# One hybrid decoder layer on one core: the MLP's two matrix products by seven products per 2x2 quad of blocks

## The chip, the core and the metric

The kernel runs on one core of a Trainium2 chip. It computes one layer of a hybrid decoder in fp32 with inputs and outputs as in the reference, in one launch. The metric is the device time of a launch in microseconds. Five engines work side by side on queues of their own: PE (TensorE, matmuls), DVE (VectorE), ACT (ScalarE), POOL (GpSimd) and SP (SyncE, here only an issuer of DMAs). They meet only in semaphores: each waits until a count is reached. Matmuls write to PSUM, eight banks of 512 fp32 columns per partition; everything else lies in SBUF.

## The reference, cut to what is touched

512 prompt tokens and 32 sample tokens (544 in all) go through the layer. After the three mixers comes

```python
x = x + mix @ w_out_l                       # w_out: 2048 x 2048, its first 512 rows belong to group A
hm = rmsnorm(x, g_mlp)
x = x + jnp.square(jax.nn.relu(hm @ w_up_l)) @ w_down_l
```

with `w_up` of 2048 x 8192 and `w_down` of 8192 x 2048, all fp32. The change touches the last part of the first line (the rows of `w_out` of group A) and the other two lines.

## The kernel before

The stages before `output_and_mlp` (the input projection in its feature-wise and token-wise form, attention, the two scans, their part of the output projection) are not touched. `output_and_mlp` (L3017) holds everything with tokens along the free axis, in two halves of 272 (`HM`), and features along partitions, 128 per tile: `x` and `h` are 16 tiles.

fp32 values go through PE as two fp32r parts: ACT writes the high part of a weight or an activation, another engine the low part (value minus high). A block product is then three matmuls per k-tile: high by high, high by low, low by high. Weights come in chunks of 2048 columns per partition, in two parts of 1024: SP loads a part into `raw` (L3084), ACT writes its high part to `ring` (`highs`, L3313), POOL its low part (`lows`, L3110), PE uses it (L3152). `ring` has two chunks.

The output projection (16 tiles, L3186) adds to `x` (DVE, L3227), multiplies by the gain (L3270), squares (ACT, L3358) and sums the squares by a matmul with ones (L3166); the high and low part of the gained tile become `h`. `rstd` is applied later, behind the up product.

The MLP runs in a hardware loop of 8 groups (`GROUPS`): 8 up chunks, which give 8 tiles of hidden features, then 8 down chunks, which add these 8 tiles' share to all 16 tiles of `x`. An up chunk is 16 k-tiles by 3 matmuls by 2 halves, so 96 matmuls of 128 x 272, and so is a down chunk (8 k-tiles, 2 output tiles). The two halves go to two banks in turn. DVE takes max(0, .) times `rstd` (L3247), ACT squares (L3337), DVE splits the hidden tile (L3235, L3237) into `hid`, which stays in SBUF. The down product is added to `x` by DVE (L3227). The order of each engine is written out by hand; SP's loads wait for `split`, ACT's highs for PE to be done with the ring's slot. At the end PE turns `x` back (L3215), DVE copies it (L3303) and ACT stores it.

## Time and profile before

| | |
|---|---|
| median of 3 runs | 3514.57 us (3513.46 to 3515.31) |
| the profiled execution | 3514.76 us, span 3512.9 us |
| output projection of group A | 1860.0 to 1928.8 us of the span |
| MLP | 1928.8 to 3493.6 us |
| turning back and storing | to 3512.9 us |
| busy: PE, DVE, ACT, POOL | 91%, 40%, 24%, 38% |

Times in a row are microseconds unless marked ns; positions count from the first instruction of the span. A row of groups gives line, engine, operation, output and inputs, shape, count, then busy time, mean ns of one, and the engine's idle time before them with what ended it. Matmuls are pipelined, so one lasts longer in the record than the distance between two starts; the same holds, less so, for DVE and ACT.

### The profile page before, as it was taken

What the parts mean: (1) busy time and instruction counts of PE and PEld (TensorE: products, weight loads), DVE (VectorE), ACT (ScalarE), POOL (GpSimd) and SP (SyncE); (2) the same over time, 40 slices, a digit from 0 to 9 for tenths busy, and PEclk for the clock granted to TensorE, in tenths of its full rate; (3) what the DMA queues carried; (4) which work ended last, traced back from release to release, by engine and by line L of the source; (5) the groups of instructions that cost most, each with busy time, mean ns of one, the idle gap of its engine ahead of it and who ended that gap; (6) DMA issues with size and microseconds to landing.
All of it is one profiled execution on the core that took longest, in us unless ns stands there. A gap on an engine that the chain in (4) does not pass through costs nothing. (4 is left out here: it accounts for less than half of the span.)

```text
span 3512.9 us, 53674 instructions
## 1 busy us (share of the span) xinstructions
PE 3205.1 (91%) x22287; PEld 2954.2 (84%) x22287; DVE 1396.2 (40%) x2390; ACT 843.7 (24%) x1376; POOL 1349.7 (38%) x852
## 2 busy tenths in 40 slices
PE   7968999999984677786998999999999999999998
PEld 6934888999763577745887999999999999999998
DVE  5026975697318665455874211111111111111112
ACT  4222222222317211224323211111121212111120
POOL 4344333475423222313334433334333343433342
PEclk9989999999995788777998999999999999999999
DMA  5322333588743000226424232222232222322222
GB/s 185 99 76 80 106 98 95 143 248 242 223 132 84 20 1 1 82 81 190 120 72 148 86 96 83 87 85 87 82 97 85 85 85 85 93 84 90 85 85 99
DMA packets 415936, 360.25 MB, mean 103 GB/s; under 512 B 26362, under 2 KB 367962, under 8 KB 414309
## 3 DMA queue, kind: packets, MB, share of 16 engines
q1 hardware_dynamic: 380368, 288.60, 28.1%
q0 software_dynamic: 13440, 42.02, 3.9%
q10 hardware_dynamic: 21888, 26.05, 2.1%
q8 instruction: 197, 3.23, 0.4%
q14 instruction: 43, 0.35, 0.0%
HBM read 311.63 MB, written 46.20 MB: 102 GB/s over the span
## 5 line engine op out<-in xcount | busy, mean ns | idle before, releaser
L3110 POOL TENSOR_TENSOR om_ring<-om_raw,om_ring 128x1024 fp32r<-128x1024 f32 x262 | 622.4, 2398 | 950.0 <-ACT om_ring L3313 950.0
L3152 PE MATMUL om_ps<-om_h,om_ring 128*128 128x272 f32 x6144 | 777.5, 289 | 16.7 <-issue 16.6
L3152 PEld LDWEIGHTS om_ps<-om_h,om_ring 128*128 128x128 f32 x6144 | 775.0, 190 | 19.1 <-issue 19.0
L3152 PE MATMUL om_ps<-om_hid,om_ring 128*128 128x272 f32 x6144 | 771.0, 288 | 0.0
L3152 PEld LDWEIGHTS om_ps<-om_hid,om_ring 128*128 128x128 f32 x6144 | 770.2, 189 | 0.0
L3313 ACT ACTIVATE om_ring<-om_raw 128x1024 fp32r<-128x1024 f32 x264 | 264.2, 1048 | 636.5 <-PE om_ps L3152 613.5
L3227 DVE TENSOR_TENSOR om_x<-om_x,om_ps 128x272 f32<-128x272 f32 x288 | 113.0, 434 | 694.8 <-PE om_ps L3152 656.3
L342 POOL TENSOR_TENSOR w_ring<-w_raw,w_ring 128x1024 fp32r<-128x1024 f32 (+2 forms) x110 | 251.7, 2308 | 345.5 <-ACT w_ring L426 345.1
L393 PE MATMUL pm_ps<-h,w_ring 128*128 128x280 f32 x2688 | 356.7, 294 | 9.1 <-issue 8.5
L393 PEld LDWEIGHTS pm_ps<-h,w_ring 128*128 128x128 f32 x2688 | 350.1, 190 | 15.5 <-issue 15.4
L3247 DVE SCALAR_TENSOR_TENSOR om_relu<-om_ps,om_rstd 128x272 f32<-128x272 f32 x128 | 50.4, 436 | 643.9 <-PE om_ps L3152 643.9
L411 PE MATMUL pm_ps<-w_ring,h 128*128 128x512 f32 (+2 forms) x1152 | 238.1, 366 | 8.0 <-POOL w_ring L342 8.0
L411 PEld LDWEIGHTS pm_ps<-w_ring,h 128*128 128x128 f32 x1152 | 200.6, 190 | 41.9 <-issue 8.0
L1961 PE MATMUL ao_w<-ao_mh,ao_ring 128*128 128x272 f32 x1152 | 180.9, 308 | 20.7 <-POOL ao_mh L2101 13.4
L3337 ACT ACTIVATE om_relu<-om_relu 128x272 f32<-128x272 f32 x128 | 49.9, 432 | 622.4 <-DVE om_relu L3247 622.4
L426 ACT ACTIVATE w_ring<-w_raw 128x1024 fp32r<-128x1024 f32 (+2 forms) x128 | 124.8, 1011 | 275.6 <-PE as_dead_bank L411 177.4
L1961 PEld LDWEIGHTS ao_w<-ao_mh,ao_ring 128*128 128x128 f32 x1152 | 156.4, 193 | 37.1 <-issue 18.4
L2111 POOL TENSOR_TENSOR ao_ring<-ao_raw,ao_ring 128x768 fp32r<-128x768 f32 x32 | 60.8, 1920 | 123.0 <-ACT ao_ring L2045 123.0
L2714 POOL DMA_INDIRECT as_rows<-in_cache_v,as_offs x64 | 64.8, 1012 | 96.1 <-PE as_o_bank L2978 81.1
L393 PEld LDWEIGHTS pi_ps<-h,w_ring 128*128 128x128 f32 x768 | 98.5, 188 | 0.1
L393 PE MATMUL pi_ps<-h,w_ring 128*128 128x280 f32 x768 | 98.5, 290 | 0.0
L2833 DVE TENSOR_TENSOR as_prod<-as_rows,as_qb 128x512 f32<-128x512 f32 x64 | 95.7, 1495 | 0.0
(527 smaller groups left out, 3515.6 us busy)
## 6 DMA issues: line engine op xcount, KB each, us to landing
om_raw<-in_w_up SPq DMA_DIRECT2D x128, 512.0 KB, 4.2
om_raw<-in_w_down SPq DMA_DIRECT2D x128, 512.0 KB, 3.7
w_raw<-in_w_in SPq DMA_DIRECT2D x112, 512.0 KB, 3.9
ao_raw<-in_w_out SPq DMA_DIRECT2D x32, 384.0 KB, 3.8
...
```

The lines of the kernel that those rows point to most:

```text
L342: eng.tensor_tensor(f32r(ring[:, n % 2, 1, half_of(q, n)]), raw[:, q, whole(q, n)], ring[:, n % 2, 0, half_of(q, n)], ALU.subtract).then_i ...
L393: ins = pe.matmul(bank_of(b + y)[:, 0:HALF], piece(a, k), f32r(h[:, x, k, two_halves(y)]), start=first, stop=last)
L411: ins = pe.matmul(bank_of(b + m)[:, 0:w], f32r(h[:, x, ld.k0 + k, tok]), piece(a, k), start=first, stop=last)
L426: act.activation(f32r(ring[:, n % 2, 0, half_of(q, n)]), raw[:, q, whole(q, n)], ACT.Copy).then_inc(hi_ready[q], 1)
L1961: ins = pe.matmul(w_ps[2 * (n % 2) + half][:, 0:HM], w, f32r(mh[:, b, k, kept_half(half)]), start=first, stop=last)
L2111: pool.tensor_tensor(f32r(ring[:, n % 2, 1, half_of(q)]), raw[:, q, :], ring[:, n % 2, 0, half_of(q)], ALU.subtract).then_inc(split[q], 1)
L2714: pool.indirect_dma_start(self.rows[:, n % RING, :], None, table, bass.IndirectOffsetOnAxis(ap=self.offs[:, x, j:j + 1], axis=0)).then_inc ...
L2833: dve.tensor_tensor(prod[:, n % 2, :], self.rows[:, n % RING, :], self.qb[:, j % 4, :], ALU.mult).then_inc(s["multiplied"], 1)
L3110: pool.tensor_tensor(f32r(ring[:, s, 1, half_of(q)]), raw[:, q, :], ring[:, s, 0, half_of(q)], ALU.subtract).then_inc(split[q], 1)
L3152: ins = pe.matmul(ps[bank][:, 0:HM], w, f32r(src[:, b, k, kept_half(half)]), start=first, stop=last)
L3227: dve.tensor_tensor(dst, dst, ps[b][:, 0:HM], ALU.add).then_inc(evac[b], 1)
L3313: act.activation(f32r(ring[:, s, 0, half_of(q)]), raw[:, q, :], ACT.Copy).then_inc(hi_ready[q], 1)
```

## The change

The weight matrices are cut into 2x2 quads of blocks, the activations into 2x2 as well: even and odd k-tiles by first and second half of the tokens. A quad's product is then made of seven block products by the scheme with 7 instead of 8 products (Winograd's form), which needs four sums of weight blocks (S1 = 21 + 22, S2 = S1 - 11, S4 = 12 - S2, and S3 = 11 - 21) and four of activation blocks per quad, and joins the products in PSUM or on DVE. There are 32 quads in the up product (`UPS`) and 8 groups of 4 in the down product (`IPS`), `QUADS` = 64. Everything is straight-line code; the loop over groups is gone. The whole up product comes first, then the whole down product.

A weight block is a piece of 1024 columns. Pieces come in the order `NAMES` (11, 12, S2, S1, S3, S4, 22). ACT writes a piece's high part and DVE, no longer POOL, its low part; `ring` has three slots of one piece. S1, S2 and S4 are made by DVE, S3 by POOL, which does nothing else. `raw` has six slots that change their roles from quad to quad, so S1 takes the place of the 12 of the quad before, and S3 that of its own 21.

In the up product ACT copies five partial sums from PSUM per quad, DVE makes three joins, applies `rstd` and max (1088 columns at once), ACT squares, DVE makes four differences, ACT and DVE split seven blocks (272 and 1632 columns), and SP stores the quad's seven split blocks to a DRAM buffer (`hid`, 1.95 MB per quad). In the down product SP loads them back by groups (`load_hidden`, seven loads of 1.11 MB per group) into the place of the activations' seven block combinations `hc`, and DVE adds every product to two tiles' halves of `x` (544 columns, `gather`). The hidden blocks of a quad pass through rows of `x`, so three quarters of `x` are stored behind the output projection and loaded again at the start of the down product. In the output projection DVE and ACT also prepare the seven combinations per pair of tiles (`combos`, `combo_lows`, `plain_highs`, `combo_highs`), all by DVE and ACT, none by POOL. The closing part is the same but for three instead of two staging buffers.

The diff, cut to its core (`done` is the product three pieces back, whose result an engine fetches before it makes piece n):

```diff
--- before.py
+++ after.py
-GROUPS, GT = 8, FF // 8 // P
-PER = GT * P // 128
+PIECE = 1024
+OUT_PIECES = D // (2 * P)
+UPS = FF // (2 * P)
+GJ = 4
+GROUPS = UPS // GJ
+IPS = D // (4 * P)
+QUADS = UPS + GROUPS * IPS
+SLOTS = 3
+NAMES = ("11", "12", "S2", "S1", "S3", "S4", "22")
+MOVES = (0, 1, 4, 3, 5, 2, 6)
+HOMES = (((0, 0), (0, 1), (1, 0), (1, 1), (4, 0), (4, 1), (3, 0)), ((5, 0), (5, 1), (2, 0), (2, 1), (6, 0), (6, 1), (3, 1)))
+H11, H12, H21, H22, HT = 0, 1, 2, 3, 4
+def piece(q, idx):
+    return OUT_PIECES + 7 * q + idx
+def raw_slots():
+    at = {"11": 2, "12": 0, "21": 1, "22": 3, "sum": 4, "spare": 5}
+    out = []
+    for _ in range(QUADS):
+        out.append(at)
+        at = {"11": at["spare"], "12": at["11"], "21": at["sum"], "22": at["21"], "sum": at["12"], "spare": at["22"]}
+    return out
...
+        def bank_of(q, idx):
+            return {1: 2, 3: 4, 5: 4}.get(idx, alpha(q))
...
+            def loads(q):
+                if q >= 2:
+                    sp.wait_ge(lo, piece(q - 2, 6) + 1)
...
+                load(q, "11")
+                sp.wait_ge(lo, piece(q - 1, 2) + 1 if q else 7)
+                load(q, "12")
+                sp.wait_ge(lo, piece(q - 1, 3) + 1 if q else 8)
+                load(q, "21")
+                if q:
+                    sp.wait_ge(lo, piece(q - 1, 4) + 1)
+                else:
+                    sp.wait_ge(prepared, 8)
+                load(q, "22")
+            def store_hidden(j):
+                sp.wait_ge(h_lo, 2 * (j + 1))
+                for a in range(2):
+                    sp.dma_start(hid[:, j // GJ, :, a, j % GJ, :], hsplit[:, a, :, :]).then_inc(hid_out, 16)
+            def load_hidden(g, c):
+                slot, half = home(g, c)
+                if g < 2:
+                    sp.wait_ge(product, 7 * (UPS - 1) + MOVES.index(slot) + 1)
+                else:
+                    sp.wait_ge(product, 7 * (UPS + IPS * (g - 1) - 1) + MOVES.index(c) + 1)
+                sp.wait_ge(hid_out, 32 * GJ * (g + 1))
+                sp.dma_start(hc[:, slot, :, GJ * half:GJ * (half + 1), :], hid[:, g, c, :, :, :]).then_inc(hid_in[g % 2][c], 16)
...
+            for q in range(QUADS):
+                loads(q)
+                if q == 0:
+                    sp.wait_ge(added, 16)
+                    sp.dma_start(x_t[:, 12:16, META:], x[:, 12:16, :]).then_inc(x_saved[3], 16)
+                if 2 <= q < UPS + 2:
+                    store_hidden(q - 2)
+                if q == UPS + 1:
+                    sp.wait_ge(x_saved[1], 16)
+                    sp.dma_start(x[:, 4:8, :], x_t[:, 4:8, META:]).then_inc(x_back[1], 16)
+                if q == UPS + 2:
+                    for part in (2, 3):
+                        sp.wait_ge(x_saved[part], 16)
+                        sp.wait_ge(hid_out, 32 * UPS)
+                        sp.dma_start(x[:, 4 * part:4 * part + 4, :], x_t[:, 4 * part:4 * part + 4, META:]
+                                     ).then_inc(x_back[part], 16)
+                if q == UPS:
+                    for c in MOVES:
+                        load_hidden(0, c)
+                g, phase = divmod(q - UPS - 1, IPS)
+                if q > UPS and g + 1 < GROUPS and phase < 3:
+                    for c in (MOVES[0:2], MOVES[2:4], MOVES[4:7])[phase]:
+                        load_hidden(g + 1, c)
...
-            def lows(n, s):
-                for q in range(PARTS):
-                    pool.wait_ge(hi_ready[q], n + 1)
-                    pool.tensor_tensor(f32r(ring[:, s, 1, half_of(q)]), raw[:, q, :], ring[:, s, 0, half_of(q)], ALU.subtract
-                                       ).then_inc(split[q], 1)
...
+            def bank_ready(q, idx):
+                up, b = q < UPS, 7 * (q - UPS)
+                if idx == 0:
+                    if q == 0:
+                        pe.wait_ge(added, KT)
+                    elif q == 1:
+                        pe.wait_ge(rooted, 1)
+                    elif q < UPS + 2:
+                        pe.wait_ge(copied, 5 * (q - 2) + 5)
+                    else:
+                        pe.wait_ge(gathered, b - 14 + 7)
+                elif idx == 1 and q:
+                    pe.wait_ge(joined, 3 * (q - 1) + 1) if q <= UPS else pe.wait_ge(gathered, b - 7 + 2)
+                elif idx == 2:
+                    pe.wait_ge(copied, 5 * q + 1) if up else pe.wait_ge(gathered, b + 1)
+                elif idx == 3 and q:
+                    pe.wait_ge(joined, 3 * (q - 1) + 3) if q <= UPS else pe.wait_ge(gathered, b - 7 + 6)
+                elif idx == 4:
+                    pe.wait_ge(copied, 5 * q + 2) if up else pe.wait_ge(gathered, b + 3)
+                elif idx == 5:
+                    pe.wait_ge(copied, 5 * q + 3) if up else pe.wait_ge(gathered, b + 4)
+                elif idx == 6:
+                    pe.wait_ge(copied, 5 * q + 4) if up else pe.wait_ge(gathered, b + 5)
+            def up_product(q, idx):
+                n, c = piece(q, idx), MOVES[idx]
+                pe.wait_ge(lo, n + 1)
+                bank_ready(q, idx)
+                for k in range(8):
+                    if q == 0 and idx == 0:
+                        pe.wait_ge(prepared, k + 1)
+                    for a, b in ((0, 0), (0, 1), (1, 0)):
+                        last = pe.matmul(ps[:, bank_of(q, idx), 0:HM], f32r(ring[:, n % SLOTS, a, P * k:P * (k + 1)]),
+                                         f32r(hc[:, c, b, k, :]), start=(idx in (0, 1, 3) and k == a == b == 0),
+                                         stop=(idx in (1, 5, 6) and k == 7 and a == 1), skip_group_check=True)
+                last.then_inc(product, 1)
+            def down_product(q, idx):
+                n, c = piece(q, idx), MOVES[idx]
+                g, ip = divmod(q - UPS, IPS)
+                slot, half = home(g, c)
+                pe.wait_ge(lo, n + 1)
+                bank_ready(q, idx)
+                if ip == 0:
+                    pe.wait_ge(hid_in[g % 2][c], 16 * (g // 2 + 1))
+                for i in range(2):
+                    for j in range(GJ):
                         for a, b in ((0, 0), (0, 1), (1, 0)):
...
+                            w = f32r(ring[:, n % SLOTS, a, 2 * P * j + P * i:2 * P * j + P * (i + 1)])
+                            last = pe.matmul(ps[:, bank_of(q, idx) + i, 0:HM], w, f32r(hc[:, slot, b, GJ * half + j, :]),
+                                             start=(idx in (0, 1, 3) and j == a == b == 0),
+                                             stop=(idx in (1, 5, 6) and j == GJ - 1 and a == 1), skip_group_check=True)
+                last.then_inc(product, 1)
...
+            def low(n):
+                dve.wait_ge(hi, n + 1)
+                dve.tensor_tensor(f32r(ring[:, n % SLOTS, 1, :]), source(n), ring[:, n % SLOTS, 0, :], ALU.subtract
+                                  ).then_inc(lo, 1)
+            def sums(q, which):
+                at = {name: raw[:, slot, :] for name, slot in slots[q].items()}
+                arrived = lambda name: dve.wait_ge(raw_in[slots[q][name]], landed[q, name])
+                if which == "S1":
+                    if q:
+                        dve.wait_ge(lo, piece(q - 1, 5) + 1)
                     else:
...
+                        dve.wait_ge(prepared, 8)
+                    arrived("21")
+                    arrived("22")
+                    dve.tensor_tensor(at["sum"], at["21"], at["22"], ALU.add).then_inc(s_done, 1)
+                elif which == "S2":
+                    dve.wait_ge(s_done, 3 * q + 1)
+                    dve.wait_ge(s3_done, q + 1)
+                    dve.wait_ge(lo, piece(q, 0) + 1)
+                    dve.tensor_tensor(at["11"], at["sum"], at["11"], ALU.subtract).then_inc(s_done, 1)
+                else:
+                    dve.wait_ge(s_done, 3 * q + 2)
+                    dve.wait_ge(lo, piece(q, 1) + 1)
+                    dve.tensor_tensor(at["12"], at["12"], at["11"], ALU.subtract).then_inc(s_done, 1)
...
+            def hidden_scaled(q):
+                dve.wait_ge(copied, 5 * q + 5)
+                dve.wait_ge(joined, 3 * q + 3)
+                both = hs[:, 0:4, :].rearrange("p (m a) t -> p m (a t)", m=2)
+                dve.scalar_tensor_tensor(out=both, in0=both, scalar=0.0, in1=bc(rstd.unsqueeze(1), [P, 2, TM]), op0=ALU.max,
+                                         op1=ALU.mult).then_inc(scaled, 1)
+            def hidden_combos(q):
+                dve.wait_ge(squared, q + 1)
+                dve.tensor_tensor(hs[:, HT, :], hs[:, H12, :], hs[:, H11, :], ALU.subtract).then_inc(h_made, 1)
...
+            def hidden_lows(q):
+                dve.wait_ge(h_hi, 2 * q + 2)
+                dve.tensor_tensor(f32r(hsplit[:, 1, 0, :]), hs[:, 0, :], hsplit[:, 0, 0, :], ALU.subtract).then_inc(h_lo, 1)
+                dve.tensor_tensor(f32r(hsplit[:, 1, 1:7, :]), hs[:, 2:8, :], hsplit[:, 0, 1:7, :], ALU.subtract
+                                  ).then_inc(h_lo, 1)
...
+            for n in range(OUT_PIECES):
+                add_tile(2 * n)
+                low(n + 2)
+                add_tile(2 * n + 1)
+                combos(n)
+                combo_lows(n)
+            for n in range(piece(0, 2), piece(QUADS, 3)):
+                q, idx = divmod(n - OUT_PIECES, 7)
+                done_q, done = divmod(n - OUT_PIECES - 3, 7)
+                if 0 <= done_q < UPS:
+                    if done in (4, 5):
+                        if done == 4:
+                            join(done_q, 1)
+                        join(done_q, done)
+                elif done_q >= UPS:
+                    gather(done_q, done)
+                if q < QUADS:
+                    if q == 0 and idx == 2:
+                        sums(0, "S1")
+                        sums(0, "S2")
+                    elif q and idx == 0:
+                        sums(q, "S1")
+                    elif q and idx == 1:
+                        sums(q, "S2")
+                    if idx == 2:
+                        sums(q, "S4")
+                if 1 <= q <= UPS and idx == 5:
+                    hidden_combos(q - 1)
+                if q < QUADS:
+                    low(n)
+                if q == 0 and idx == 4:
+                    dve.wait_ge(rooted, 1)
+                    dve.reciprocal(rstd, rstd).then_inc(rstd_ready, 1)
+                    dve.wait_ge(rstd_ready, 1)
+                if 1 <= q <= UPS and idx == 3:
+                    hidden_scaled(q - 1)
+                if 1 <= q <= UPS and idx == 6:
+                    hidden_lows(q - 1)
...
+        @block.gpsimd
+        def _(pool):
+            for q in range(QUADS):
+                at = {name: raw[:, slot, :] for name, slot in slots[q].items()}
+                pool.wait_ge(s_done, 3 * q + 1)
+                pool.wait_ge(raw_in[slots[q]["11"]], landed[q, "11"])
+                pool.tensor_tensor(at["21"], at["11"], at["21"], ALU.subtract).then_inc(s3_done, 1)
...
+            def high(n):
+                slot_free(act, n)
+                source_ready(act, n)
+                act.activation(f32r(ring[:, n % SLOTS, 0, :]), source(n), ACT.Copy).then_inc(hi, 1)
...
+            for n in range(OUT_PIECES):
+                square(2 * n)
+                high(n + 2)
+                square(2 * n + 1)
+                plain_highs(n)
+                combo_highs(n)
+            act.wait_ge(summed, KT)
+            act.activation(rstd.rearrange("p (a t) -> p a t", a=2), ps[:, 6:8, 0:HM], ACT.Sqrt, bias=sb["eps"][:, 0:1],
+                           scale=1.0 / D).then_inc(rooted, 1)
+            for n in range(piece(0, 2), piece(QUADS, 3)):
+                q, idx = divmod(n - OUT_PIECES, 7)
+                done_q, done = divmod(n - OUT_PIECES - 3, 7)
+                if 0 <= done_q < UPS and done in (0, 2, 3, 4, 6):
+                    copy_out(done_q, done)
+                if q < QUADS:
+                    high(n)
+                if 1 <= q <= UPS and idx == 4:
+                    hidden_squares(q - 1)
+                if 1 <= q <= UPS and idx == 5:
+                    hidden_highs(q - 1)
```

## Rows read from the trace of the kernel before

**Rows 1.** The page: busy time of each engine, and the clock by slices.

```profile
PE 3205.1 (91%) x22287; PEld 2954.2 (84%) x22287; DVE 1396.2 (40%) x2390; ACT 843.7 (24%) x1376; POOL 1349.7 (38%) x852
PEclk9989999999995788777998999999999999999999
```

**Rows 2.** Stretches: from:to, length, busy of each engine (x instructions), PEclk, DMA share, GB/s.

```profile
2125.00:2320.00 195.00, 192.90 (x1532) 192.69 (x1531) 30.05 (x80) 37.47 (x48) 74.71 (x33) 0.99 0.29 87
```

**Rows 3.** Waits in 1929 to 3493: engine, line, awaited, us in total, times, longest.

```profile
DVE om_x L3227 <- PE om_ps L3152: 656.3, 128, 5.2
...
PE om_ps L3152 <- issue: 16.6, 10, 2.3
```

**Rows 4.** PE in order of time: start, length, what, idle before.

```profile
1859.98 11.26 PE L3186 MATMUL om_ps<-om_h,om_ring 128*128 128x272 f32 x72 [14.50 <-POOL om_h L3116]
...
1890.83 1.08 PE L3166 MATMUL om_ps<-om_tile,ones 128*128 128x272 f32 x4
...
1894.76 1.08 PE L3166 MATMUL om_ps<-om_tile,ones 128*128 128x272 f32 x4
...
1928.85 96.57 PE L3152 MATMUL om_ps<-om_h,om_ring 128*128 128x272 f32 x768
2025.26 96.37 PE L3152 MATMUL om_ps<-om_hid,om_ring 128*128 128x272 f32 x768
2123.63 98.01 PE L3152 MATMUL om_ps<-om_h,om_ring 128*128 128x272 f32 x768 [2.00 <-issue]
...
2319.94 2.51 PE L3152 MATMUL om_ps<-om_h,om_ring 128*128 128x272 f32 x18 [2.10 <-issue]
...
3493.58 7.18 PE L3215 MATMUL om_ps<-ident,om_x 128*128 128x128 f32 x64 [0.84 <-DVE om_x L3227]
```

**Rows 5.** A stretch of L411 alone, columns PE and PEld, clock, DMA share, GB/s.

```profile
60.00:70.00 10.00, 10.00 (x45) 8.16 (x44) 1.00 0.14 35
```

**Rows 6.** DVE: two of 1024 and of 272 columns in a row, then means of one.

```profile
888.45 2.36 DVE L342 TENSOR_TENSOR w_ring<-w_raw,w_ring 128x1024 fp32r<-128x1024 f32 x2 [6.81 <-ACT w_ring L426]
1941.14 0.79 DVE L3247 SCALAR_TENSOR_TENSOR om_relu<-om_ps,om_rstd 128x272 f32<-128x272 f32 x2 [2.37 <-PE om_ps L3152]
...
L342 DVE TENSOR_TENSOR w_ring<-w_raw,w_ring 128x1024 fp32r<-128x1024 f32 x18 | 21.3, 1220 | 95.9 <-ACT w_ring L426 78.9 <-issue 17.0
L3247 DVE SCALAR_TENSOR_TENSOR om_relu<-om_ps,om_rstd 128x272 f32<-128x272 f32 x128 | 50.4, 436 | 643.9 <-PE om_ps L3152 643.9
```

**Rows 7.** ACT: two of 1024 and of 272 columns, and a hand-off to DVE.

```profile
1935.01 2.00 ACT L3313 ACTIVATE om_ring<-om_raw 128x1024 fp32r<-128x1024 f32 x2
1941.62 0.78 ACT L3337 ACTIVATE om_relu<-om_relu 128x272 f32<-128x272 f32 x2 [4.60 <-DVE om_relu L3247]
...
874.37 1.06 ACT L426 ACTIVATE w_ring<-w_raw 128x1024 fp32r<-128x1024 f32 x1 [5.03 <-DMA w_raw<-in_w_in]
875.56 1.23 DVE L342 TENSOR_TENSOR w_ring<-w_raw,w_ring 128x1024 fp32r<-128x1024 f32 x1 [4.14 <-ACT w_ring L426]
```

**Rows 8.** A DVE product alone and beside POOL; POOL's 1024 columns (mean ns).

```profile
783.76 0.68 DVE L2833 TENSOR_TENSOR as_prod<-as_rows,as_qb 128x512 f32<-128x512 f32 x1
785.08 5.88 DVE L2833 TENSOR_TENSOR as_prod<-as_rows,as_qb 128x512 f32<-128x512 f32 x1
785.68 4.73 POOL L342 TENSOR_TENSOR w_ring<-w_raw,w_ring 128x1024 fp32r<-128x1024 f32 x2
...
L3110 POOL TENSOR_TENSOR om_ring<-om_raw,om_ring 128x1024 fp32r<-128x1024 f32 x262 | 622.4, 2398 | 950.0 <-ACT om_ring L3313 950.0
```

**Rows 9.** DMA: a stretch while x is loaded, and the landing of a weight load.

```profile
1864.00:1866.00 2.00, 2.00 (x16) 2.00 (x16) 0.78 (x2) 0.00 (x0) 0.00 (x0) 0.90 1.06 390
om_raw<-in_w_up SPq DMA_DIRECT2D x128, 512.0 KB, 4.2
```

**Rows 10.** Stretches as in rows 2: behind the gap at 2121, and behind that at 2318.

```profile
2125.00:2126.00 1.00, 1.00 (x6) 1.00 (x6) 0.00 (x0) 0.00 (x0) 1.00 (x2) 0.50 0.00 0
2323.00:2325.00 2.00, 2.00 (x18) 2.00 (x18) 0.00 (x0) 0.00 (x0) 0.83 (x1) 1.00 0.86 245
```

518 lines of the change are left out of this document (256 added, 262 removed).

## The prediction

> **What bounds the kernel now.** I read the page's busy times first [rows 1], then the stages [rows 2], then who waits for whom in the MLP [rows 3], and last TensorE's own order of time [rows 4]. The page says PE 91% busy, every other engine at most 40%. In the MLP a stretch of 195 us holds 193 us of PE at full clock, with DVE at 30 us, ACT at 37 and POOL at 75. The waits agree: DVE waited 656 us for PE; PE waited 16.6 us in all, for "issue". So PE sets the end. 768 matmuls take 96.37 us with the tail of the last; their starts are 0.1253 us apart. Out of 1564.7 us between the first MLP matmul (1928.85) and the first transpose (3493.58) the 12288 matmuls are 1539.7. The other 25 lie at the group loop's seven boundaries, about 2 us of "issue" each, after some of which the clock drops.
>
> **PE's side of the change.** A quad of 2x2 blocks needed 8 block products and now needs 7: 8 k-tiles by 3 split terms by 7 are 168 matmuls of the same shape, where the same 256 rows and 544 tokens took 192. 64 quads make 10752, which is 1536 fewer: -192.4 us. A product lasts 24 x 0.1253 = 3.01 us, a quad 21.04, all 64 1346.8. The loops are gone, and straight-line PE code elsewhere shows no such gaps, so the 25 us go too. One thing is new to this stage: the 12 or 24 matmuls in a row that go to one bank, where before two banks alternated. The input projection's token-wise branch (L411) already sends 12 in a row of 512 columns to one bank and does 45 in 10 us, 0.222 us each [rows 5]. That is 9 ns over the columns' own 0.213 at 2.4 GHz, where the 272-column matmuls show 12 over 0.113. So I cost it at nothing; that row bounds it closely from both sides.
>
> **What the other engines must do in a quad.** Two DVE operations of 1024 columns take 2.36 us, one 1.22: starts are 1.14 us apart, and for 272 columns 0.36 (0.79 less 0.43) [rows 6]. A line through both gives 0.64 for 544, 1.21 for 1088 and 1.77 for 1632 (estimates). ACT: 0.95 for 1024, 0.35 for 272, so 1.0 for 1088 and 1.44 for 1632 [rows 7]. From an ACT end to the DVE start that waits for it 0.13 us pass (875.43 to 875.56) [rows 7].
> The weight lows move from POOL to DVE. In an up quad DVE does 7 lows and 3 sums (10 x 1.14), 3 joins (1.08), the scaling (1.21), 4 differences of the hidden blocks (1.44) and the hidden lows (0.36 + 1.77): 17.3 us. In a down quad it is 10 x 1.14 and 7 gathers of 0.64: 15.9. POOL does one sum, 2.40 us [rows 8].
> POOL and DVE get in each other's way. A DVE product of two SBUF tiles takes 0.68 us alone; one that meets two POOL operations (4.73 us) takes 5.88, 5.20 more [rows 8]. DVE stood still for as long as POOL worked, and a little over. So POOL's 2.40 go on DVE's time in each quad where both want to work. The bounds are 0 (POOL meets only DVE's idle time) and 2.6 (half of 5.20); I take 2.40, POOL's own length, as that row is near it.
> Down quads then have 18.3 of 21.04 us, and a ring of three slots lets DVE run two products (6 us) ahead: hidden. Up quads have 19.7, so what counts is the order.
>
> **An up quad in DVE's order**, every operation starting when its engine is free and its last wait is met; t = 0 at S1. S1 to 1.14, low 11 to 2.29. POOL, ready at 1.35, gets in when that low is through, 2.29 to 4.69. DVE meanwhile has only a 0.36 join and waits 2.17 for S3. S2 at 4.82, low 12 at 5.96, S4 at 7.22 (it waits 0.12 for its predecessor's end), the lows of S2 and S1 at 8.36 and 9.50, the scaling at 10.64, low S3 at 11.85. The differences wait for ACT's square (12.06 to 13.15), start at 13.29 and are through at 15.0; low S4 15.12. ACT then splits the hidden blocks (0.35 + 1.44), copies a bank (0.35) and only then makes the high of 22 (17.2 to 18.2), so its low starts at 18.36, after 2.10 of waiting. Hidden lows 19.5 to 21.6, two joins, next S1 at 22.47. Work 17.26 and waits 5.2: the ring of DVE, POOL and ACT closes in 22.47 us without any wait for PE, which needs 21.04. PE then waits 1.43 us in each up quad, at its second product, for low 12. The Trainium skill (VectorE: DVE Perf Modes, "The DRAIN you can't avoid") says that after every operation the next starts only when the pipe is empty. The pair of [rows 6] shows starts 1.14 apart with 1.22 of length, so the measurement decides; by that sentence the ring would be about 1.5 us longer (0.08 for each of 19 operations), +45 us in all.
>
> **The stages.** (a) Output projection. PE needs 3.93 us per tile (1890.83 to 1894.76), 62.8 in all, and before took 68.9 (1859.98 to 1928.85) [rows 4]. Now ACT and DVE work by pairs of tiles on one chain: add, square, base copy, four dependent differences, ACT's split, its low (1.21), the next add, its square, ACT's high and the low of the weights: 0.73 + 0.7 + 0.5 + 1.7 + 1.4 + 1.2, then 0.85 + 0.7 + 1.1 + 1.2, about 10.1 us per pair where PE needs 7.86. The first two tiles (7), eight such chains (80.8) and less the last one's tail (3.3), behind whose first parts the MLP already starts: 84.5 us, +15.6.
> (b) First up quad: S1, S2 and S4 can start only after the last preparation (buffers shared with it), with POOL's 2.4 between. PE waits 8.4 us before its third product and 1.7 for the last tile of the first: +10.0.
> (c) 30 further up quads' stalls: +43 (30 x 1.43).
> (d) Turn to the down product: the first group's hidden blocks, 7 x 1.11 MB, go out only behind the store of hidden 30 (1.95 MB). At the 390 GB/s that the load of x reached [rows 9] the first lands 7.0 us late, each next one in 2.9, under a product's 3.0. The weights of the second down quad stand behind them: +4.0 and +2.4. Sum +13.4.
> (e) Down quads: none, +1.1 at the last gather.
> (f) Clock. After two of the gaps of some 2 us the clock is 0.5 for 3.4 us, and the stretch took 98.01 us instead of 96.57; after that of 2319 it stayed up [rows 4, 10]. I charge 8 us for the gaps of (a), (b) and (d), most of one such loss for each, and none for the stalls of 1.43 us in (c), which are shorter than any gap of these rows.
> Everything before L3017, and the 19.3 us of transposes and stores behind it, stay. DMA: before 86 GB/s in the MLP. Per quad now 2.1 MB of weights and 1.95 MB of hidden blocks, first out and later in: 192 GB/s of the 390, and DVE needs the last weight block 6 us after its issue where one lands in 4.2 [rows 9]: nothing.
>
> **Sum.** -192.4 - 25.2 + 15.6 + 10.0 + 43 + 13.4 + 1.1 + 8 = -126.5; walked through without rounding, -127.2. The profiled execution is 3514.76 us (span 3512.9), 0.2 over the median of 3514.57. So 3387.6 by its time, 3387.4 against the median: I say 3388.
>
> **Rivals.** (1) *The up quads run at PE's pace.* If POOL's sum meets no DVE work (DVE is idle for 2.2 us around it) and hand-offs are shorter, the ring falls to 21.3: -1.2 x 30 = -36, and most of (f): 3345. For it: 5.2 us of DVE's ring are waits. Against: DVE's low follows S1 at once, so the two meet each time. Chance 0.20.
> (2) *The stalls cost the clock.* The Trainium skill (TensorE: Matmul & The Clock Gate, "A second HAM failure mode: psum-queue depth-cycling") tells of a kernel whose short idle times between groups made the clock swing. As a mechanism here: each of the 30 stalls drops the clock as the gap at 2121 did [rows 4, 10], 1.44 us each: +43, 3431. Against: 1.4 us is shorter than the gaps seen, and one shown there cost nothing. By that rule of the Trainium skill the swing would be the rule here too; the rows show one gap with it and one without. Chance 0.17.
> (3) *Slower than before.* The same stall, but the half clock holds on. The gain of 127 us is used up when an up quad takes 4.2 us more, so when PE is at 1.2 GHz for over 8.4 us of it. At four of seven products (12 us): +6.0 x 30 = +180, 3568. For it: the middle of the profile has slices at 0.5 and 0.7 [rows 1], 88 us each. Against: PE is nearly idle there, and here it would be 94% busy. Chance 0.05.
> The forecast (ring of 22 to 23 us) keeps 0.56, 3365 to 3410. The last 0.02 is for a transfer or buffer that I have missed.
> **Range.** 3345 (rival 1) to 3433 (just over rival 2), which leaves out rival 3 and the tails. This kernel's runs differ by 0.05%, and about 0.2% can be told from no change. Faster 0.93, same 0.01, slower 0.06.
>
> **What would show it.** In the profile of the changed kernel: 10752 MLP matmuls, 0.125 us apart; DVE near 85% busy in the up stage; PE's starts per up quad 22.5 us apart with one wait per quad, for DVE's low, at the second product; the down stage without waits, 21.04 per quad; DVE waiting for POOL's sum once a quad; some 7 us of PE waiting for a DMA at the turn; full clock in the up stage. It would be wrong if DVE's wait for POOL were absent (rival 1), if PEclk showed 0.5 every quad (2, 3), or if PE waited for DMA in every quad.

## The result, and the profile after

The changed kernel takes 3374.97 us (median of 4 runs, 3372.2 to 3379.66), the kernel before 3514.02 beside it: ratio 0.961 with a 95% interval of 0.959 to 0.963, faster by 139 us. The prediction was 3388, range 3345 to 3433. The profiled execution has a span of 3373.4 us (3375.16 with what lies around it).

The page of the changed kernel: busy times, TensorE's clock by slices; then groups (line, engine, operation, names, shapes, count | busy us, mean ns | idle before them).

```profile
PE 3037.0 (90%) x20751; PEld 2771.9 (82%) x20751; DVE 2270.1 (67%) x2961; ACT 1165.6 (35%) x1713; POOL 924.1 (27%) x643
PEclk9989999999996588957999999999999999999999
...
L3278 PE MATMUL om_ps<-om_hc,om_ring 128*128 128x272 f32 x5376 | 688.6, 290 | 27.6 <-DVE om_ring L3326 27.6
L3295 PE MATMUL om_ps<-om_hc,om_ring 128*128 128x272 f32 x5376 | 685.3, 290 | 12.1 <-DMA om_hc<-hid_scratch 6.6 <-DVE om_ring L3326 2.6 <-DVE om_x L3438 2.5
```

Against [rows 1], PE has 1536 matmuls less and 168 us less to do, and is still 90% busy. DVE has taken over the weight lows: 1396 to 2270 us. The up product (L3278) and the down product (L3295) have the 10752 matmuls predicted, and PE waits 27.6 and 12.1 us in them.

PE in order of time (start, length, what, idle before), the changed kernel, as in [rows 4]:

```profile
1856.60 11.22 PE L3241 MATMUL om_ps<-om_hc,om_ring 128*128 128x272 f32 x72 [15.41 <-DVE om_ring L3326]
...
1886.59 1.19 PE L3225 MATMUL om_ps<-om_small,ones 128*128 128x272 f32 x4 [1.72 <-ACT om_small L3515]
...
1941.14 7.32 PE L3278 MATMUL om_ps<-om_hc,om_ring 128*128 128x272 f32 x48
1957.08 40.92 PE L3278 MATMUL om_ps<-om_hc,om_ring 128*128 128x272 f32 x312 [8.62 <-DVE om_ring L3326]
...
2219.63 21.45 PE L3278 MATMUL om_ps<-om_hc,om_ring 128*128 128x272 f32 x168 [0.62 <-DVE om_ring L3326]
2241.69 21.45 PE L3278 MATMUL om_ps<-om_hc,om_ring 128*128 128x272 f32 x168 [0.62 <-DVE om_ring L3326]
...
2663.91 21.12 PE L3295 MATMUL om_ps<-om_hc,om_ring 128*128 128x272 f32 x144 [6.59 <-DMA om_hc<-hid_scratch]
2685.22 3.26 PE L3295 MATMUL om_ps<-om_hc,om_ring 128*128 128x272 f32 x24 [0.20 <-issue]
2689.65 3.29 PE L3295 MATMUL om_ps<-om_hc,om_ring 128*128 128x272 f32 x24 [1.17 <-DVE om_ring L3326]
2694.35 3.29 PE L3295 MATMUL om_ps<-om_hc,om_ring 128*128 128x272 f32 x24 [1.41 <-DVE om_ring L3326]
2697.98 127.80 PE L3295 MATMUL om_ps<-om_hc,om_ring 128*128 128x272 f32 x1008 [0.34 <-DVE om_x L3438]
...
3355.52 8.95 PE L3318 MATMUL om_ps<-ident,om_x 128*128 128x128 f32 x80 [0.81 <-DVE om_x L3438]
```

The output projection lasts 84.54 us (1856.60 to 1941.14); PE waits about every 10 us there, for ACT's squares. Then comes one wait of 8.62 us before the third product. The rows 2219.63 and 2241.69 are two of 29 of their kind: an up quad every 22.07 us, with one wait, for DVE. At the turn to the down product PE waits for the first hidden blocks and then for DVE, and after that for almost nothing: the last two rows are 657.5 us apart.

What DVE and POOL do at the start of an up quad:

```profile
2230.38 1.23 DVE L3326 TENSOR_TENSOR om_ring<-om_raw,om_ring 128x1024 fp32r<-128x1024 f32 x1 [1.80 <-ACT om_ring L3509]
...
2234.57 1.22 DVE L3339 TENSOR_TENSOR om_raw<-om_raw 128x1024 f32<-128x1024 f32 x1
2235.71 1.22 DVE L3326 TENSOR_TENSOR om_ring<-om_raw,om_ring 128x1024 fp32r<-128x1024 f32 x1
2235.87 3.32 POOL L3502 TENSOR_TENSOR om_raw<-om_raw 128x1024 f32<-128x1024 f32 x1 [18.75 <-DVE om_raw L3339]
2236.84 0.43 DVE L3404 TENSOR_TENSOR om_x<-om_ps,om_small 128x272 f32<-128x272 f32 x1
2239.28 1.23 DVE L3344 TENSOR_TENSOR om_raw<-om_raw 128x1024 f32<-128x1024 f32 x1 [2.00 <-POOL om_raw L3502]
2240.42 1.22 DVE L3326 TENSOR_TENSOR om_ring<-om_raw,om_ring 128x1024 fp32r<-128x1024 f32 x1
2241.69 0.52 PE L3278 MATMUL om_ps<-om_hc,om_ring 128*128 128x272 f32 x2 [0.62 <-DVE om_ring L3326]
```

POOL's sum (L3502) has a length of 3.32 us, where 1024 columns took 2.40 [rows 8]: it begins beside DVE's low and gets its turn when that low is through (2236.93). S2 (L3344) waits 2.00 us for it, the low behind S2 is the low of 12, and PE's wait ends when that one ends.

### The profile page after: what moved, and what is told of

Read it like the earlier page. It is cut to its first block and busy times, and to the rows that moved or that the text cites. A ratio compares the mean times of both kernels' runs of the same rounds, so it can differ in the third digit from the quotient of the medians.

```text
span 3373.4 us, 51215 instructions
## 1 busy us (share of the span) xinstructions
PE 3037.0 (90%) x20751; PEld 2771.9 (82%) x20751; DVE 2270.1 (67%) x2961; ACT 1165.6 (35%) x1713; POOL 924.1 (27%) x643
## 5 line engine op out<-in xcount | busy, mean ns | idle before, releaser
L3278 PE MATMUL om_ps<-om_hc,om_ring 128*128 128x272 f32 x5376 | 688.6, 290 | 27.6 <-DVE om_ring L3326 27.6
L3278 PEld LDWEIGHTS om_ps<-om_hc,om_ring 128*128 128x128 f32 x5376 | 681.5, 189 | 34.7 <-DVE om_ring L3326 34.4
L3509 ACT ACTIVATE om_ring<-om_raw 128x1024 fp32r<-128x1024 f32 x456 | 482.7, 1059 | 656.1 <-PE om_ps L3295 349.2
L3295 PE MATMUL om_ps<-om_hc,om_ring 128*128 128x272 f32 x5376 | 685.3, 290 | 12.1 <-DMA om_hc<-hid_scratch 6.6
L3295 PEld LDWEIGHTS om_ps<-om_hc,om_ring 128*128 128x128 f32 x5376 | 681.6, 189 | 15.8 <-DVE om_ring L3326 10.2
L3326 DVE TENSOR_TENSOR om_ring<-om_raw,om_ring 128x1024 fp32r<-128x1024 f32 x456 | 554.3, 1221 | 110.3 <-ACT om_ring L3509 110.1
L3502 POOL TENSOR_TENSOR om_raw<-om_raw 128x1024 f32<-128x1024 f32 x64 | 211.2, 3300 | 1297.6 <-DVE om_raw L3339 1297.6
L411 PE MATMUL pm_ps<-w_ring,h 128*128 128x512 f32 (+2 forms) x1152 | 237.3, 365 | 8.0 <-POOL w_ring L342 8.0
L411 PEld LDWEIGHTS pm_ps<-w_ring,h 128*128 128x128 f32 x1152 | 199.9, 189 | 41.9 <-issue 8.1
L3438 DVE TENSOR_TENSOR om_x<-om_x,om_ps 128x544 f32<-128x544 f32 x224 | 160.9, 718 | 75.9 <-PE om_ps L3295 75.4
L3344 DVE TENSOR_TENSOR om_raw<-om_raw 128x1024 f32<-128x1024 f32 x64 | 78.5, 1226 | 117.7 <-POOL om_raw L3502 117.7
L453 ACT ACTIVATE pm_stage<-pm_ps 128x280 f32<-128x280 f32 (+3 forms) x80 | 35.6, 445 | 239.6 <-PE pm_ps L393 189.1
L740 DVE SCALAR_TENSOR_TENSOR conv_y<-conv_x,conv_par,conv_y 128x616 f32<-128x616 f32 x84 | 71.3, 859 | 36.4 <-ACT conv_y L667 34.3
```

The costliest lines, as they stand in the source:

```text
L411: ins = pe.matmul(bank_of(b + m)[:, 0:w], f32r(h[:, x, ld.k0 + k, tok]), piece(a, k), start=first, stop=last)
L3278: last = pe.matmul(ps[:, bank_of(q, idx), 0:HM], f32r(ring[:, n % SLOTS, a, P * k:P * (k + 1)]), f32r(hc[:, c, b, k, :]), start=(idx in (0 ...
L3295: last = pe.matmul(ps[:, bank_of(q, idx) + i, 0:HM], w, f32r(hc[:, slot, b, GJ * half + j, :]), start=(idx in (0, 1, 3) and j == a == b == 0),
L3326: dve.tensor_tensor(f32r(ring[:, n % SLOTS, 1, :]), source(n), ring[:, n % SLOTS, 0, :], ALU.subtract).then_inc(lo, 1)
L3344: dve.tensor_tensor(at["11"], at["sum"], at["11"], ALU.subtract).then_inc(s_done, 1)
L3438: dve.tensor_tensor(dst, dst, ps[:, b:b + 2, 0:HM], ALU.add).then_inc(gathered, 1)
```

## The experiments

They ran in three sets, on different chips, where the kernel before took 3510.89, 3496.39 and 3501.06 us. So ratios to the kernel before of the same set are compared, and rows of the profiles.

| kernel | median us | ratio | 95% interval |
|---|---|---|---|
| changed kernel | 3374.97 | 0.961 | 0.959 to 0.963 |
| the same again (after_again) | 3363.29 | 0.961 | 0.959 to 0.963 |
| before_one_bank | 3512.14 | 1.001 | 1.000 to 1.002 |
| low12_first | 3368.31 | 0.959 | 0.958 to 0.961 |
| s3_on_dve | 3342.2 | 0.952 | 0.950 to 0.954 |
| pool_more | 3404.05 | 0.969 | 0.968 to 0.971 |
| pool_in_four | 3379.13 | 0.965 | 0.964 to 0.967 |
| front_order | 3344.7 | 0.956 | 0.954 to 0.958 |
| turn_order | 3360.24 | 0.961 | 0.959 to 0.963 |
| banks_in_turn | 3355.83 | 0.960 | 0.959 to 0.962 |
| no_round_trip | 3346.8 | 0.957 | one run |
| gains_pool_sum | 3326.89 | 0.950 | 0.949 to 0.952 |
| all_gains | 3309.13 | 0.946 | 0.944 to 0.947 |

**The theory** was that DVE, POOL and ACT form a ring that closes in about 22 us, where PE needs 21, because POOL's sum and DVE keep each other out. **The rival** was that the up quads lose their time elsewhere. Its simplest test takes POOL out.

```diff
                 elif which == "S2":
                     dve.wait_ge(s_done, 3 * q + 1)
+                    arrived("11")
+                    dve.tensor_tensor(at["21"], at["11"], at["21"], ALU.subtract).then_inc(s3_done, 1)
                     dve.wait_ge(s3_done, q + 1)
...
-                pool.tensor_tensor(at["21"], at["11"], at["21"], ALU.subtract).then_inc(s3_done, 1)
```

> The fourth sum S3 is made by DVE too, POOL does nothing in the MLP. Ring theory with POOL and DVE excluding each other: the 2.0 us wait for POOL goes, 1.14 of work comes, the ring falls to 21.2 us and PE (168 x 0.1267 = 21.3) sets the up quad: 30 x 0.78 = 23 us less, 3352; down quads unchanged. Rival (DVE's amount of work sets the up quad, POOL relieves it): 1.14 us more per up quad, 30 x 1.14 = +34, 3409.

Measured 0.952. PE's order of time, all four sums on DVE:

```profile
1951.44 675.05 PE L3278 MATMUL om_ps<-om_hc,om_ring 128*128 128x272 f32 x5328 [6.38 <-DVE om_ring L3326]
2633.08 20.33 PE L3295 MATMUL om_ps<-om_hc,om_ring 128*128 128x272 f32 x144 [6.59 <-DMA om_hc<-hid_scratch]
...
2666.75 651.13 PE L3295 MATMUL om_ps<-om_hc,om_ring 128*128 128x272 f32 x5160 [0.34 <-DVE om_x L3440]
```

The up product is one run of 5328 matmuls with no wait, and by its matmul starts a quad takes 21.23 us instead of 22.07. DVE has one operation more per quad and the kernel is faster. The up part became 25 us shorter (23 expected). That the down part also became 6 us shorter was not expected. In the changed kernel an unstalled down quad takes 21.19 us, but 11 of the 30 quads from the third on take 0.1 to 0.8 us more, 5.7 us in all, at their second and third products. In each of these 11, S1 (L3339) had waited 0.48 to 1.20 us for its weights, and the quad lost that wait less 0.35 to 0.38 us. The waits of the changed kernel and of no_round_trip (below), which keeps POOL's sum but moves less data:

```profile
DVE om_raw L3339 <- DMA om_raw<-in_w_down: 12.4, 14, 2.1
...
DVE om_raw L3339 <- DMA om_raw<-in_w_down: 1.2, 1, 1.2
```

So two things have to meet: weights that land late and POOL's sum on the way from S1 to S2. Without POOL's sum S1 still waits, 9 times between 2710 and 3320 us, and only one quad loses time, 0.16 us; with POOL's sum but without most of the traffic, one loses 0.8 and no other any.

**Which way around the ring.** If POOL's length is what counts, giving DVE other work meanwhile (the low of 12 ahead of S2, which does not need S3) gains little.

```diff
-                    elif q and idx == 1:
-                        sums(q, "S2")
...
                     low(n)
+                    if q and idx == 1:
+                        sums(q, "S2")
```

> DVE makes the low part of block 12 ahead of the sum S2, for which it waits for POOL; nothing else changes. Ring theory (the up quad's 22.07 us are the closed ring of DVE, POOL and ACT; PE's own need is 21.3): the low has two SBUF inputs and so stands still while POOL works, the ring keeps its length, up quads stay at 22.07 us and the time at 3375; PE's wait only changes its place. Rival (PE is held up by that one low): its wait of 0.6 us at the second product goes, up quads take 21.3, 30 x 0.78 = 23 us less: 3352.

Measured 21.86 us per up quad, 0.21 less, where the theory expected none and the rival 0.78. DVE and POOL in that kernel:

```profile
2213.18 1.22 DVE L3326 TENSOR_TENSOR om_ring<-om_raw,om_ring 128x1024 fp32r<-128x1024 f32 x1
2213.34 3.31 POOL L3502 TENSOR_TENSOR om_raw<-om_raw 128x1024 f32<-128x1024 f32 x1 [18.55 <-DVE om_raw L3339]
2214.31 0.43 DVE L3404 TENSOR_TENSOR om_x<-om_ps,om_small 128x272 f32<-128x272 f32 x1
2214.66 3.07 DVE L3326 TENSOR_TENSOR om_ring<-om_raw,om_ring 128x1024 fp32r<-128x1024 f32 x1
2217.66 1.21 DVE L3344 TENSOR_TENSOR om_raw<-om_raw 128x1024 f32<-128x1024 f32 x1
```

The low ahead of S2 takes 3.07 us instead of 1.22: it stands still until POOL ends at 2216.65, and 1.1 us later it is done. DVE's wait for POOL's semaphore became a stop at POOL's operation. The join (L3404), which reads PSUM and a small tile, ran its usual 0.43 beside it.

**How much of a POOL operation counts.** Five more POOL products of 128 columns per quad, on tiles that nothing else needs in the MLP, with no DVE operation waiting for them:

```diff
+                pool.wait_ge(s_done, 3 * q + 3)
+                pool.wait_ge(rooted, 1)
+                for i in range(5):
+                    pool.wait_ge(spun, 5 * q + i)
+                    pool.tensor_tensor(sb["ones"][:, :], sb["ident"][:, :], sb["ident"][:, :], ALU.mult).then_inc(spun, 1)
```

> POOL does five extra products of 128 columns per quad after S4 (about 0.45 to 0.5 us each, 2.4 in all), into a tile nobody reads in the MLP; no engine waits for them. Exclusion theory: DVE's two-input operations stand still for those 2.4 us, the ring becomes 24.4 us: +2.4 x 31 = +73, and down quads (18.3 + 2.4 of 21.3 us) 0 to +10: 3448 to 3458. Rival (POOL costs DVE only the wait for S3): no change, 3375.

Measured 0.969, or 29 us more, and up quads of 22.93 us (+0.87): neither theory's number. DVE and POOL in that kernel:

```profile
2185.36 5.96 POOL L3508 TENSOR_TENSOR ones<-ident 128x128 f32<-128x128 f32 x5 [3.86 <-DVE om_raw L3348]
2187.68 1.48 DVE L3410 SCALAR_TENSOR_TENSOR om_x<-om_x,om_small 128x1088 f32<-128x1088 f32 x1
...
2190.42 0.63 DVE L3415 TENSOR_TENSOR om_x<-om_x 128x272 f32<-128x272 f32 x1
```

DVE's scaling takes 1.48 us where it took 1.29, a difference of the hidden blocks 0.63 for 0.44: each POOL operation costs DVE 0.19 to 0.20. And POOL's five need 5.96 us, 1.19 each: each ends 0.26 us after the DVE operation that it stood behind. The two take turns by whole operations, and what DVE loses is not POOL's whole length but what POOL still has to do when DVE's next operation starts (0.34 us here), less 0.14; neither theory had that. The low of low12_first fits as well: POOL had 1.99 us left at its start, and it took 1.85 longer. The next kernel asks it directly, with the low of 12 ahead of S2 and POOL's sum cut in four (the waits for it count four times as far):

```diff
-                pool.tensor_tensor(at["21"], at["11"], at["21"], ALU.subtract).then_inc(s3_done, 1)
+                for c in range(4):
+                    s = slice(256 * c, 256 * (c + 1))
+                    pool.tensor_tensor(at["21"][:, s], at["11"][:, s], at["21"][:, s], ALU.subtract).then_inc(s3_done, 1)
```

> POOL's sum in four pieces of 256 columns instead of one of 1024, and DVE's low of 12 ahead of its sum S2, so that two lows run beside POOL's pieces. In the kernel with the low ahead and POOL's sum in one piece, the low took 3.07 us beside it instead of 1.22, and the five small POOL operations of another run stretched DVE's by 0.2 us each. Theory (the engines exclude each other for as long as a POOL operation really works, 0.6 to 0.75 us for 256 columns): the lows take 1.9 to 2.0 us beside each piece, DVE loses as much in all, POOL ends later for the four starts, up quads of 21.9 to 22.4 us. Rival (a small POOL operation costs DVE some 0.2 us, whatever its length, and the two take turns): the lows take under 1.5 us each beside POOL, and quads fall to 21.3 to 21.6 us.

DVE and POOL in that kernel:

```profile
2207.84 1.22 DVE L3326 TENSOR_TENSOR om_ring<-om_raw,om_ring 128x1024 fp32r<-128x1024 f32 x1
2208.00 4.72 POOL L3504 TENSOR_TENSOR om_raw<-om_raw 128x256 f32<-128x256 f32 x4 [17.63 <-DVE om_raw L3339]
2208.98 0.43 DVE L3404 TENSOR_TENSOR om_x<-om_ps,om_small 128x272 f32<-128x272 f32 x1
2209.33 1.41 DVE L3326 TENSOR_TENSOR om_ring<-om_raw,om_ring 128x1024 fp32r<-128x1024 f32 x1
...
2212.82 1.23 DVE L3344 TENSOR_TENSOR om_raw<-om_raw 128x1024 f32<-128x1024 f32 x1 [2.08 <-issue]
```

Each theory got one number right. The low beside the pieces takes 1.41 us, not 3.07 or 1.9 (the rival's "under 1.5"): the first piece has 0.33 us left when it starts, again 0.14 more than it loses; but the quads are 22.35 us apart, inside the theory's 21.9 to 22.4. The four pieces together take 4.72 us instead of 3.31: the first two are 1.66 and 1.72 long, since each waits through a DVE low, the last two 0.74 each with DVE idle. What DVE no longer loses by standing still, it loses by waiting 2.08 us for the later S3. The exclusion costs whichever engine has to stand back, and here both ways end at S2.

**The cadence of the matmuls.** In the changed kernel matmuls within a product start 0.1261 us apart, where the kernel before had 0.1253. I had costed sending 12 or 24 in a row to one bank at nothing. The kernel before with the halves as an outer loop does that (and uses the same weights for two matmuls in a row instead of four):

```diff
-                for m in range(cols // P):
+                for m, half in ((m, half) for m in range(cols // P) for half in range(2)):
```

> The kernel before with the halves as the outer loop of a chunk, so that each bank gets its 24 or 48 matmuls in a row and every matmul has other weights than the one before; same matmuls, same count. If one bank in a row (or new weights each time) is why the MLP matmuls now start 0.1267 instead of 0.1253 us apart: 12288 x 0.0013 = +16 us, 3531. Rival (the cadence comes from the heavier DMA and DVE traffic): starts stay 0.1253 us apart, 3514.

1.0006 (0.9996 to 1.0015), starts 0.1256 apart: 0.3 ns of the 0.8. The change's own down product with its two banks in turn, instead of one after the other:

```diff
-                for i in range(2):
-                    for j in range(GJ):
-                        for a, b in ((0, 0), (0, 1), (1, 0)):
+                for j in range(GJ):
+                    for a, b in ((0, 0), (0, 1), (1, 0)):
+                        for i in range(2):
```

> In the down product the two output tiles of a k-tile alternate, so that every matmul goes to the other bank than the one before, with the same moving data twice; same matmuls. After the one-bank run of the kernel before (0.1256 us from 0.1253) I expect of the banks 0.3 ns of the 0.9 by which starts lie further apart than before: down starts at 0.1258, 2 us less, which the total does not show: 3373. If the banks are the whole cause: 0.1253, 5 us less. If traffic is: 0.1261 as now.

Starts in the down product 0.1251 apart instead of 0.1261, and the stage from 2647.64 to 3333.11 takes 685.5 us instead of 691.6. The ratio, 0.960 against 0.961, does not tell 6 us from nothing by itself; the rows do. So in the down product this order of the loop is the whole of the 0.8 ns and 0.2 more, while in the kernel before the swap gave 0.3. That it is the banks is not shown: each of the two edits also changes the order of the operands. Here two matmuls in a row had the same weights, and now none have, while the same moving tile comes twice in a row. No kernel here separates the two.

**The stages with a one-time cost.** In the output projection DVE and ACT put the tile that PE waits for first, ahead of the ring's low and after the ring's high:

```diff
                 add_tile(2 * n)
-                low(n + 2)
                 add_tile(2 * n + 1)
+                low(n + 2)
...
-                square(2 * n)
                 high(n + 2)
+                square(2 * n)
                 square(2 * n + 1)
```

> In the output projection DVE adds both tiles of a pair before it makes the low part of the weights, and ACT makes the weights' high part ahead of the squares. Chain theory (DVE and ACT hand each other the work by pairs in 9.8 us where PE needs 7.8): the square, the high and the low leave the chain, a pair takes PE's 7.8, and the stage falls from 84.5 to about 71 us: 13 less, 3362. Rival (PE waits because DVE is short of time in this stage): its work is unchanged, so the stage stays at 84 and the time at 3375.

0.956 against 0.961, and by the rows the projection takes 67.1 us instead of 84.5:

```profile
1843.87 11.27 PE L3241 MATMUL om_ps<-om_hc,om_ring 128*128 128x272 f32 x72 [15.12 <-DVE om_ring L3326]
...
1910.95 3.01 PE L3278 MATMUL om_ps<-om_hc,om_ring 128*128 128x272 f32 x21
```

The chain of about 10 us per pair was a matter of order, not of work: all 15.6 us that the prediction charged there were to be had back. 17 us came back where I expected 13; how much of it is DVE's swap and how much ACT's is not separated.

At the turn, the loads of the first hidden blocks go ahead of the last-but-one store:

```diff
+                if q == UPS:
+                    for c in MOVES:
+                        load_hidden(0, c)
                 if 2 <= q < UPS + 2:
                     store_hidden(q - 2)
...
-                if q == UPS:
-                    for c in MOVES:
-                        load_hidden(0, c)
```

> At the turn from the up to the down product SP issues the first group's seven loads of hidden blocks ahead of the store of hidden 30. Queue theory (the first load stands behind 1.95 MB of stores, 5 us at 390 GB/s): PE's wait for the first load falls from 6.6 to about 2 us, 5 less in all: 3370. Rival (the load waits for its own buffer, that is for PE): 6.6 us stay, 3375.

No difference in the ratio. PE's order of time in that kernel:

```profile
2645.31 3.19 PE L3295 MATMUL om_ps<-om_hc,om_ring 128*128 128x272 f32 x24
2649.12 15.49 PE L3295 MATMUL om_ps<-om_hc,om_ring 128*128 128x272 f32 x120 [0.62 <-DVE om_ring L3326]
2671.35 11.79 PE L3295 MATMUL om_ps<-om_hc,om_ring 128*128 128x272 f32 x72 [6.74 <-issue]
```

The wait for the first block is gone, and one of 6.74 us has come six products later: from the end of the up product to the transposes it is 695.1 us instead of 698.2. "issue" hides what ended it; ACT and DVE in the same stretch show it:

```profile
2664.41 0.43 ACT L3558 ACTIVATE om_x<-om_x 128x272 fp32r<-128x272 f32 x1 [7.78 <-DMA hid_scratch<-om_x]
...
2667.27 1.23 DVE L3326 TENSOR_TENSOR om_ring<-om_raw,om_ring 128x1024 fp32r<-128x1024 f32 x1 [7.08 <-ACT om_ring L3509]
...
2670.54 0.71 DVE L3438 TENSOR_TENSOR om_x<-om_x,om_ps 128x544 f32<-128x544 f32 x1
```

ACT may split the last hidden blocks only when the store of hidden 30 has left their place. That store now stands behind the 7.8 MB of loads, so ACT waits 7.78 us for it; ACT's highs, DVE's low and DVE's gather (L3438) come later by as much, and PE goes on when that gather is done. The edit moved the wait from the loads to the store; a store that goes between the loads was not tried. That the wait comes from transfers shows with the round trip cut down (one of seven stored blocks and an eighth of each load are kept, so most hidden values that the down product reads are left out):

```diff
-sp.dma_start(hid[:, j // GJ, :, a, j % GJ, :], hsplit[:, a, :, :])
+sp.dma_start(hid[:, j // GJ, 0:1, a, j % GJ, :], hsplit[:, a, 0:1, :])
...
-sp.dma_start(hc[:, slot, :, GJ * half:GJ * (half + 1), :], hid[:, g, c, :, :, :])
+sp.dma_start(hc[:, slot, 0:1, GJ * half:GJ * half + 1, :], hid[:, g, 0, 0:1, 0:1, :])
```

> One seventh of each hidden store and one eighth of each hidden load are left, the rest is left out (the down product then works on old blocks, so the output is not the reference's); waits and order stay. DMA goes from 192 to about 110 GB/s. If the traffic is why the MLP matmuls start 0.9 ns further apart: 0.1253, 8 us less, and with PE's waits at the turn gone (6.6 and 2.8) 3358. If it is not: only the turn's 9 us, 3366.

PE waits 0.62, 0.80, 0.64, 0.34 and 0.33 us at the turn there, and the up quads are 22.07 us apart as before: the round trip costs its 7 us at the turn and nothing in the up stage. Behind the turn PE has no wait left, though POOL makes its sum:

```profile
2697.39 629.78 PE L3295 MATMUL om_ps<-om_hc,om_ring 128*128 128x272 f32 x4992 [0.33 <-DVE om_x L3438]
```

Its matmuls start 0.1261 apart, so the transfers are not what stretches them.

**All together.** The changed kernel again, and two kernels with the gains combined: all_gains has s3_on_dve, front_order, turn_order and banks_in_turn; gains_pool_sum has low12_first in the place of s3_on_dve.

> The changed kernel itself, unaltered, for a comparison on the same chip with the three kernels beside it, since the time of the kernel before differed by 14 us between the earlier sets of runs (3510.89 and 3496.39). Expected: a ratio to the kernel before of 0.961 within 0.002, quads of the up product 22.07 us apart, matmuls of the down product 0.1262 us apart.

> The same with the one change that POOL keeps its sum per quad, DVE's low of 12 going ahead of its sum S2: what is left against the kernel with all four sums on DVE is then the price of POOL's work. Theory (POOL's sum holds DVE's ring, 30 up quads of 21.86 us where PE needs 21.2): 20 us slower in the up stage and level in the down stage, 3375 - 6 - 17 - 3 - 6 = 3343, ratio 0.952. Rival (the gain of moving the sum was the one-time wait before the third product and the smoother down stage, not the ring): ratio below 0.949 and up quads under 21.5 us.

> Four edits together: all four weight sums on DVE, the preparation's new order on DVE and ACT, the loads of the first hidden blocks issued ahead of the store of hidden 30, and the two banks in turn in the down product. If each gain lies in a stretch of its own they add up: 32 us for the sums, 17 for the preparation, 6 for the banks, 3 for the turn; but of the sums' 32, some 6 were waits of 0.2 us per quad in the down stage that two banks in turn could hide or lay bare again, since PE is then faster. Expected 3375 - 52 to 58 = 3317 to 3323, ratio 0.945 to 0.947. Rival: with PE waiting for nothing, DVE's own work of 19 to 20 us per down quad (11 operations of 1.14, 7 gathers) comes within 1 us of PE's 21.0 and PE waits again for DVE: ratio 0.950, with waits for DVE in the down stage. At no time should an up quad take over 21.3 us.

Measured 0.961, 0.950 and 0.946. The changed kernel has up quads of 22.07 us again; gains_pool_sum has 21.86, the theory's number and not the rival's under 21.5. PE's order of time in all_gains:

```profile
1926.97 675.68 PE L3278 MATMUL om_ps<-om_hc,om_ring 128*128 128x272 f32 x5328 [7.43 <-DVE om_ring L3326]
2602.49 18.35 PE L3295 MATMUL om_ps<-om_hc,om_ring 128*128 128x272 f32 x144
2629.27 138.16 PE L3295 MATMUL om_ps<-om_hc,om_ring 128*128 128x272 f32 x1080 [8.42 <-issue]
2767.65 519.30 PE L3295 MATMUL om_ps<-om_hc,om_ring 128*128 128x272 f32 x4152 [0.22 <-DVE om_x L3440]
```

After its first 15 us the MLP has one long wait left, at the turn: 8.42 us, while ACT waits 9.39 us for the store of hidden 30, as in turn_order. From the first matmul of the output projection to the transposes it is 1442.9 us against 1498.9 in the changed kernel: 56 less, in the 52 to 58 expected. The rival (DVE as the bound of the down stage) is out: 5232 matmuls, 0.22 us of waiting. Of the two, the kernel that leaves POOL its sum is 17.8 us slower (20 expected); its down stage, expected level, is 3.8 us longer in the profiled executions. all_gains, at 0.946, is the best of the case.

## Why the prediction was right

The sign, the mechanism and the size came out. The sum did so partly by luck: steps that were too long by 23 us and others too short by 11 leave 12. By its steps, in us of the profiled executions (predicted span 3512.9 - 127.2 = 3385.7, measured 3373.4, so 12.3 too long; waits are taken from start to start, beyond the usual step):

| step | predicted | measured | error |
|---|---|---|---|
| start of the output projection | 1859.98 | 1856.60 | -3.4 |
| (a) output projection | 84.5 | 84.5 | 0.0 |
| (b) waits of the first up quad | 10.0 | 9.6 | -0.4 |
| (c) each of 30 up quads | 22.47 | 22.07, the first 22.41 | -11.7 |
| (d) waits at the turn | 13.4 | 11.0 | -2.4 |
| (e) each of the 34 other quads | 21.04 | 21.19 | +5.1 |
| (e) waits in the 30 last down quads | 0 | 5.7 | +5.7 |
| (e) last gather | 1.1 | 1.0 | -0.1 |
| (f) clock | 8 | 4.2 | -3.8 |
| transposes and stores | 19.3 | 17.9 | -1.4 |

They add up to -12.4. The first is no part of the change: in front_order the same instruction starts at 1843.87.

**The ring** (c) was the argument that decided between 3345 and 3388, and it held to 2%. The order is as walked through: the low first, POOL when it is through, S2 4.71 us after S1 (4.82 predicted), DVE's second wait at ACT's high of 22. That wait was 1.80 us, not 2.10. Set beside the walk-through, DVE is 0.11 us ahead at S2, 0.23 at the differences, 0.48 at the low of 22 and 0.40 at the next S1. s3_on_dve showed the cause: take POOL's sum away, and the ring is faster than PE, though DVE does more.

**The cadence** failed as a step: [rows 5], 512 columns in a row to one bank, did not bound the 272-column matmuls. It cost little, for a reason the prediction did not see: in an up quad PE has slack. Its 168 matmuls need 21.19 us, not 21.04, and 0.1 more where the first one behind a wait is slow; the wait shrinks by as much (0.62 us on the row, 0.78 from start to start beyond the usual step, where 1.43 were predicted), and the quad stays 22.07. Only the quads in which PE is the bound pay.

**"Down quads: none"** and the "nothing" for DMA were nearly right, and failed together. Weight loads that the prediction let land in 4.2 us took 5.4 in the median of the down stage; S1 waited for them in 13 of the quads there, and where it waited over 0.4 us, POOL's sum behind it left no room to catch up: 5.7 us. "A ring of three slots lets DVE run two products ahead" holds for weights, not for the sum S2 that waits for POOL. The loads between 2700 and 3350 us (count, KB, median us to landing):

```profile
om_raw<-in_w_down SPq DMA_DIRECT2D x117, 512.0 KB, 5.4
```

**The turn** was right in kind and in its first term (6.59 against 7.0); the lows of the second quad's weights came 1.17 and 1.41 us late instead of 4.0 and 2.4.

**The clock.** Rival 2 did not happen: over one whole up quad with its stall the granted clock was full. The columns: stretch, length, busy PE, PEld, DVE, ACT and POOL, clock, DMA share, GB/s.

```profile
2219.63:2241.69 22.06, 21.44 (x168) 21.22 (x168) 17.77 (x20) 11.64 (x16) 3.32 (x1) 1.00 0.64 184
...
1957.00:1960.00 3.00, 2.92 (x13) 2.92 (x14) 3.00 (x4) 0.94 (x1) 0.00 (x0) 0.50 0.46 133
...
2664.00:2668.00 4.00, 4.00 (x18) 4.00 (x19) 0.00 (x0) 0.00 (x0) 0.00 (x0) 0.50 1.02 416
```

Behind the waits of 8.62 and 6.59 us it was at 1.2 GHz, its lower level, and matmuls started 0.227 us apart: 11 of them behind the one, 25 behind the other, 5 at the start of the MLP, at 0.1 us each and with the ones half in it 4.2 in all. DVE is 17.77 of 22.06 us busy, 81% where I wrote near 85. The Trainium skill's rule on short idle times (TensorE: Matmul & The Clock Gate, "A second HAM failure mode: psum-queue depth-cycling") did not come out here: 29 stalls of 0.62 us, one every 22.07 us, left the clock at full. Nor did rival 3 come near: to use up the whole gain of 139 us the 30 up quads would have had to take over 4 us more each.
